# Delta branch of a hybrid mixer kernel: the two 64 x 64 squares of a block's diagonal stored side by side

## What is computed

```
G = cumsum(g) ; decay = where(j <= i, exp(G_i - G_j), 0)
m = where(j < i, (k*beta) k^T * decay, 0) ; a = m + I           # 64 x 64
u, w = solve_triangular(a, [v*beta, k*beta*exp(G)])             # unit lower
attn = (q k^T) * decay                                          # 64 x 64
per chunk: v_new = u - w S ; o = q exp(G) S + attn v_new ; S = S exp(G_last) + k_tail^T v_new
```

## Time and profile before

| what | value |
|---|---|
| median of 3 runs | 1843.88 us (1841.74 to 1844.7) |
| the profiled execution: its time | 1846.73 us |
| the profiled execution: its span, first to last instruction | 1844.9 us |
| mean granted TensorE clock | 0.997 |
| VectorE busy | 1250.9 us, 68% |
| ScalarE busy | 952.7 us, 52% |
| GpSimd busy | 315.0 us, 17% |
| HBM read | 302.90 MB, 165 GB/s over the span |

### The profile page before, as it was taken

The page is one execution under the profiler, slowest core; times in us unless marked ns, Lnnn a source line. Parts: engine busy times, 40 slices in busy tenths (PEclk is TensorE's granted clock), DMA queues, the critical chain, the costliest instruction groups (busy, mean ns, idle before and its releaser), DMA issues.

```text
span 1844.9 us, 37214 instructions
## 1 busy us (share of the span) xinstructions
PE 1805.4 (98%) x15880; PEld 1714.5 (93%) x15880; DVE 1250.9 (68%) x1668; ACT 952.7 (52%) x1377; POOL 315.0 (17%) x174
## 2 busy tenths in 40 slices
PE   7999999999999999999999999999999999999998
PEld 7889998998888999999989999999999889999998
DVE  6885677665689648777648775587647795677643
ACT  5634466544554345564545445556534545556533
POOL 0050231000002303200001453320001352321000
PEclk9999999999999999999999999999999999999999
DMA  6453354656445334655665563456655654445663
GB/s 242 154 167 104 124 174 157 204 193 210 154 149 172 116 115 140 203 177 180 195 196 169 192 206 126 138 178 199 202 191 174 224 188 131 140 168 195 195 196 102
DMA packets 91524, 315.54 MB, mean 171 GB/s; under 512 B 11616, under 2 KB 12768, under 8 KB 91104
## 3 DMA queue, kind: packets, MB, share of 16 engines
q1 hardware_dynamic: 90784, 312.60, 52.3%
q10 hardware_dynamic: 576, 0.57, 0.1%
HBM read 302.90 MB, written 1.05 MB: 165 GB/s over the span
## 4 chain that ended last, share of the span: by engine, by line
PE 84%; DVE 12%; ACT 3%; issue 1%; DMA 0%; SPq 0%; DVEq 0%; ACTq 0%
PE bank L2019 82%; DVE wlo L1144 4%; DVE area L1144 3%; DVE area L1150 2%; ACT area L648 1%; ACT whi L654 1%; PE bank L2613 1%; DVE hl L1150 1%; DVE xT L1150 1%; DMA raw<-in_weights 0%; DVE area L1664 0%; DVE area L1662 0%; PE bank L2634 0%; PE bank L2253 0%; ACT L636 0%
## 5 line engine op out<-in xcount | busy, mean ns | idle before, releaser
L1144 DVE TENSOR_TENSOR wlo<-raw,whi 128x1024 fp32r<-128x1024 f32 x514 | 665.7, 1309 | 388.3 <-ACT whi L654 387.6
L2019 PE MATMUL bank<-hh,whi 128*128 128x256 f32 x2896 | 818.6, 284 | 23.8 <-DVE wlo L1144 18.7
L2019 PE MATMUL bank<-hh,wlo 128*128 128x256 f32 x2906 | 802.1, 277 | 0.0
L2019 PE MATMUL bank<-hl,whi 128*128 128x256 f32 x2896 | 794.4, 278 | 0.0
L654 ACT CAST whi<-raw 128x1024 fp32r<-128x1024 f32 x568 | 585.3, 1047 | 373.3 <-PE bank L2019 324.1
L2019 PEld LDWEIGHTS bank<-hh,whi 128*128 128x128 f32 x2896 | 545.6, 188 | 40.5 <-DVE wlo L1144 23.1
L2019 PEld LDWEIGHTS bank<-hh,wlo 128*128 128x128 f32 x2906 | 546.3, 188 | 0.0
L2019 PEld LDWEIGHTS bank<-hl,whi 128*128 128x128 f32 x2896 | 541.6, 189 | 1.5 <-issue 1.4
L1800 POOL TENSOR_TENSOR area<-area 128x512 f32<-128x512 f32 (+4 forms) x84 | 138.3, 1652 | 535.4 <-ACT area L648 213.3
L1800 POOL TENSOR_TENSOR wlo<-raw,whi 128x1024 fp32r<-128x1024 f32 x54 | 138.4, 2564 | 385.2 <-ACT whi L654 385.2
L2019 PE MATMUL bank<-FH,whi 128*128 128x256 f32 x640 | 177.4, 277 | 0.0
(11 more groups left out here) (132 smaller groups left out, 1905.9 us busy)
## 6 DMA issues: line engine op xcount, KB each, us to landing
raw<-in_weights SPq DMA_DIRECT2D x568, 512.0 KB, 4.1
area<-area SPq DMA_DIRECT2D x100, 64.0 KB, 3.8
area<-area SPq DMA_DIRECT2D x16, 128.0 KB, 4.0
cst<-in_const SPq DMA_DIRECT2D x1, 1188.0 KB, 8.1
cst<-in_const SPq DMA_DIRECT2D x1, 1024.5 KB, 5.8
xT<-in_x SPq DMA_DIRECT2D x4, 256.0 KB, 7.3
out<-xT SPq DMA_DIRECT2D x4, 256.0 KB, 2.8
area<-in_lev SPq DMA_DIRECT2D x2, 384.0 KB, 6.9
```

What stands on the lines that cost most here:

```text
L1144: return v.tensor_tensor(dst, x, y, op)
L2019: return e.matmul(ps, x, y, start=start, stop=stop, skip_group_check=skip)
```

## The change

The 64 x 64 squares of the seven tiles are stored with both squares of a block in the same 64 columns: square 0 in partitions 0 to 63, square 1 in partitions 64 to 127, block b in columns 64b to 64b+63. Eight blocks take 512 columns: one PSUM bank and half a tile. Every VectorE and ScalarE operation on those tiles now covers 512 columns, and the pairs of operations over j become one with one wait. The exception is the first difference out of the `cums` banks, which keep blocks of 128 columns: there two operations of 128 x 512 become four of 64 partitions x 256 columns. Matmuls of the groups are the same in number, size and order, with other addresses; their 16 results go to one bank, and they signal once in place of once per half. `KT`, `KB`, `VB`, `W` and `U` keep their form. The masks are stored in the same way; of the six transposed level masks only the first, the one that is used, is still loaded, so the constant transfer shrinks from 1188 KB to 128 x 1800 fp32 and each load of the level masks from 128 x 768 to 128 x 384 fp32. No instruction changes its place on any engine's list.

The diff, cut to its core:

```diff
+def cells(t):
+    return t[:, 0:512]
+def v8(t):
+    return t[:, 0:512].rearrange("p (b t) -> p b t", t=64)
...
 # ScalarE
-                act(DT[:, :], DT[:, :], AF.Exp).then_inc(*a_dn.up("decay", L))
+                act(cells(DT), cells(DT), AF.Exp).then_inc(*a_dn.up("decay", L))
...
-                for j in range(2):
-                    a.wait_ge(*e_dn.at("MT", L, j))
-                    a.copy(pair(MT, j), bank[j][:, :]).then_inc(*a_dn.up("MT", L, j))
+                a.wait_ge(*e_dn.at("MT", L))
+                a.copy(cells(MT), bank[0][:, :]).then_inc(*a_dn.up("MT", L))
...
-                        for j in range(2):
-                            a.wait_ge(*e_dn.at("XT", L, s, j))
-                            a.copy(pair(Y, j), bank[2 + j][:, :]).then_inc(*a_dn.up("Y", L, s, j))
+                        a.wait_ge(*e_dn.at("XT", L, s))
+                        a.copy(cells(Y), bank[2][:, :]).then_inc(*a_dn.up("Y", L, s))
...
 # VectorE
-                    tt(quarter(pair(DT, j)), quarter(bank[j]), wide(G_[:, 4 * j:4 * j + 4], 2, 128), OP.subtract).then_inc(*v_dn.up("d", L, j))
+                    for q in range(2):
+                        r = slice(64 * q, 64 * q + 64)
+                        x = tt(v8(DT)[r, 4 * j:4 * j + 4, :], quarter(bank[j])[r, :, r], wide(G_[r, 4 * j:4 * j + 4], 2, 64), OP.subtract)
+                    x.then_inc(*v_dn.up("d", L, j))
...
-                tt(v3(DT, 128), v3(DT, 128), wide(C("upper"), 1, 8), OP.mult).then_inc(*v_dn.up("diff", L))
+                tt(v8(DT), v8(DT), wide(C("tri"), 1, 8), OP.mult).then_inc(*v_dn.up("diff", L))
...
-                for j in range(2):
-                    v.wait_ge(*e_dn.at("KK", L, j))
-                    tt(quarter(pair(M, j)), quarter(bank[j]), wide(be[:, 4 * j:4 * j + 4], 2, 128), OP.mult).then_inc(*v_dn.up("m", L, j))
-                    v.wait_ge(*v_dn.now())
-                    v.wait_ge(*e_dn.at("DT", L, j))
-                    tt(pair(M, j), pair(M, j), bank[2 + j][:, :], OP.mult).then_inc(*v_dn.up("M", L, j))
+                v.wait_ge(*e_dn.at("KK", L))
+                tt(v8(M), v8(bank[0]), wide(be, 2, 64), OP.mult).then_inc(*v_dn.up("m", L))
+                v.wait_ge(*v_dn.now())
+                v.wait_ge(*e_dn.at("DT", L))
+                tt(cells(M), cells(M), bank[2][:, :], OP.mult).then_inc(*v_dn.up("M", L))
...
-                tt(v3(X, 128), v3(M, 128), wide(lev(0), 1, 8), OP.mult).then_inc(*v_dn.up())
+                tt(v8(X), v8(M), wide(lev(0), 1, 8), OP.mult).then_inc(*v_dn.up())
...
-                    for j in range(2):
-                        v.wait_ge(*e_dn.at("LX", L, s, j))
-                        tt(quarter(pair(T0, j)), quarter(bank[j]), wide(lev(s), 1, 4), OP.mult).then_inc(*v_dn.up("T0", L, s, j))
+                    v.wait_ge(*e_dn.at("LX", L, s))
+                    tt(v8(T0), v8(bank[0]), wide(lev(s), 1, 8), OP.mult).then_inc(*v_dn.up("T0", L, s))
...
-                    for j in range(2):
-                        v.wait_ge(*e_dn.at("XLX", L, s, j))
-                        tt(pair(t, j), pair(t, j), bank[b + j][:, :], OP.subtract).then_inc(*v_dn.up("X", L, s, j))
+                    v.wait_ge(*e_dn.at("XLX", L, s))
+                    tt(cells(t), cells(t), bank[b][:, :], OP.subtract).then_inc(*v_dn.up("X", L, s))
...
 # TensorE
+            def cell(t, b, q):
+                return t[64 * q:64 * q + 64, 64 * b:64 * b + 64]
-            def sub_blocks(name, x, y, b0):
-                for j in range(2):
-                    for b in range(4 * j, 4 * j + 4):
-                        for q in range(2):
-                            o = mm(sub(bank[b0 + j], b % 4, q), sub(x, b, q), sub(y, b, q), True, True, True)
-                    o.then_inc(*e_dn.up(*name, j))
+            def sub_blocks(name, x, y, to):
+                for b in range(8):
+                    for q in range(2):
+                        o = mm(cell(bank[to], b, q), cell(x, b, q), cell(y, b, q), True, True, True)
+                o.then_inc(*e_dn.up(*name))
...
```

More of the change, by code:

```diff
@@ L43 @@
     ("ones", 128), ("eye", 128), ("eps6", 1), ("eps5", 1), ("one", 1), ("pad", 1),
-    ("upper", 128), ("chunk", 128), ("levT", 6 * 128),
+    ("upper", 128), ("chunk", 128), ("levT", 64), ("tri", 64), ("unit", 64),
     ("cos", 256), ("sin", 256), ("rmask", 4 * 128), ("xi", 4 * 64), ("zeta", 4), ("cnt", 4 * 16), ("cntw", 4)])
@@ L377, in program @@
         SM = slot(16)
-        LEV = SM[:, 256:1024]
+        LEV = SM[:, 256:640]
         Z = slot(17)
@@ L1279, in delta @@
                 v.wait_ge(*v_dn.now())
[L1280 removed]
+                tt(v8(X), v8(M), wide(lev(0), 1, 8), OP.mult).then_inc(*v_dn.up())
                 v.wait_ge(*v_dn.now())
[L1282 to L1284 removed]
+                stt(v8(X), v8(X), -1.0, wide(C("unit"), 1, 8), OP.mult, OP.add).then_inc(*v_dn.up("X", L, 0))
+                v.wait_ge(*a_dn.at("MT", L))
+                tt(v8(Y), v8(MT), wide(C("levT"), 1, 8), OP.mult).then_inc(*v_dn.up())
                 v.wait_ge(*v_dn.now())
[L1286 removed]
+                stt(v8(Y), v8(Y), -1.0, wide(C("unit"), 1, 8), OP.mult, OP.add).then_inc(*v_dn.up("Y", L, 0))
                 yield 1
[L1288 to L1290 removed]
+                v.wait_ge(*e_dn.at("KQ", L))
+                tt(cells(AT), cells(DT), bank[2][:, :], OP.mult).then_inc(*v_dn.up("AT", L))
                 yield 1
                 for s in range(1, 6):
[L1293 to L1295 removed]
+                    v.wait_ge(*e_dn.at("LX", L, s))
+                    tt(v8(T0), v8(bank[0]), wide(lev(s), 1, 8), OP.mult).then_inc(*v_dn.up("T0", L, s))
                     yield 1
@@ L2265, in sub, with sub_turned, sub_scores @@
                 return t[64 * q:64 * q + 64, 128 * b + 64 * q:128 * b + 64 * q + 64]
-            def sub_turned(name, src, b0):
-                for j in range(2):
-                    for b in range(4 * j, 4 * j + 4):
-                        for q in range(2):
-                            x = mm(sub(bank[b0 + j], b % 4, q), sub(src, b, q), sub(C("eye"), 0, q), True, True, True)
-                    x.then_inc(*e_dn.up(*name, j))
-            def sub_blocks(name, x, y, b0):
-                for j in range(2):
-                    for b in range(4 * j, 4 * j + 4):
-                        for q in range(2):
-                            o = mm(sub(bank[b0 + j], b % 4, q), sub(x, b, q), sub(y, b, q), True, True, True)
-                    o.then_inc(*e_dn.up(*name, j))
[L2283 to L2290, removed]
+            def cell(t, b, q):
+                return t[64 * q:64 * q + 64, 64 * b:64 * b + 64]
+            def sub_turned(name, src, to):
+                for b in range(8):
+                    for q in range(2):
+                        x = mm(cell(bank[to], b, q), cell(src, b, q), sub(C("eye"), 0, q), True, True, True)
+                x.then_inc(*e_dn.up(*name))
+            def sub_blocks(name, x, y, to):
+                for b in range(8):
+                    for q in range(2):
+                        o = mm(cell(bank[to], b, q), cell(x, b, q), cell(y, b, q), True, True, True)
+                o.then_inc(*e_dn.up(*name))
+            def sub_scores(name, x, y, to):
+                for b in range(8):
+                    for q in range(2):
+                        c = slice(128 * b + 64 * q, 128 * b + 64 * q + 64)
+                        o = mm(cell(bank[to], b, q), x[:, c], y[:, c], True, True, True)
+                o.then_inc(*e_dn.up(*name))
             def fresh2(b0, event):
@@ L2359, in delta @@
                         r = slice(64 * q, 64 * q + 64)
-                        x = mm(bank[q][:, 64 * b:64 * b + 64], KB[r, 128 * b:128 * b + 128], sub(Y, b, q), True, True, True)
+                        x = mm(bank[q][:, 64 * b:64 * b + 64], KB[r, 128 * b:128 * b + 128], cell(Y, b, q), True, True, True)
                         if b == 7:
@@ L2367, in delta @@
                             r, c = slice(64 * q, 64 * q + 64), 128 * (b % 4)
-                            x = mm(bank[2 + j][r, c:c + 128], sub(Y, b, q), VB[r, 128 * b:128 * b + 128], True, True, True)
+                            x = mm(bank[2 + j][r, c:c + 128], cell(Y, b, q), VB[r, 128 * b:128 * b + 128], True, True, True)
                     x.then_inc(*e_dn.up("U", L, j))
@@ L2404, in delta @@
                         for d in (0, 64):
-                            x = mm(place(h)[d:d + 64, :], hv(VN)[r, h, d:d + 64], AT[r, 128 * b + 64 * q:128 * b + 64 * q + 64], n == 0, True, True)
+                            x = mm(place(h)[d:d + 64, :], hv(VN)[r, h, d:d + 64], AT[r, 64 * b:64 * b + 64], n == 0, True, True)
                     x.then_inc(*e_dn.up("o", L, n))
@@ L2676, in levels, with cells_of @@
     return [(p // (2 << s) == f // (2 << s)) & (p // (1 << s) % 2 == 1) & (f // (1 << s) % 2 == 0) for s in range(6)]
+def cells_of(a):
+    return np.concatenate([a[0:64, 0:64], a[64:128, 64:128]], 0)
 def constants1():
@@ L2695, in constants1 @@
     put("chunk", same)
-    lev = levels()
```

(6 more changed lines are left out.)

36 lines of the change are left out of this document (18 added, 18 removed).

## The result

| kernel | median | runs |
|---|---|---|
| before | 1843.85 us | 1841.74 to 1844.7 |
| changed | 1872.72 us | 1871.44 to 1873.57 |

The ratio is 1.016, with a 95% interval of 1.0147 to 1.0172: the change makes the kernel slower by 29 us, where 8 us less was forecast. The profiled execution has a span of 1870.2 us and a mean granted clock of 0.999.

A forecast was written before the change was run, and what follows sets the result against it. VectorE was taken to bound layer 0's delta branch until 112.9 us, then TensorE's weight matmuls. Stalls and tails of 3.96 + 4.15 us, together 8.1, off the median 1843.88 gave 1835.8 us; range 1833.5 to 1840.0.

The forecast's parts named there:

- The stall and its removal: TensorE waits 2.58 us before `XLX` of level 1 in both layers; with slow-clock tails 8.1 us, all to go.
- the critical `T0`: VectorE's mask of `T0` at level 1, for which TensorE waits; to end 5.6 us earlier, 3.1 us spare.
- the rule on the shared ports: GpSimd and two-SBUF-input VectorE operations take turns; second subtraction would end at 107.0 us, `T0` at 108.8, 1.6 us spare.
- the two stretches: 114 to 116 and 598 to 600 us, behind the stalls; TensorE's granted clock to rise from 0.50 to 1.00.
- The four operations of 64 x 256: VectorE's first difference, four operations replacing two of 128 x 512: 1.64 us against 1.19, adding 0.45 us.
- The sum of 8.1 us: Stalls and slow-clock tails on TensorE, 3.96 us in layer 0 plus 4.15 in layer 1, all saved.
- 8.1 + 2 us off: The largest saving in the range of 8 in 10, whose lower end was given as 1833.5 us.
- the row: Profile times of VectorE's subtractions: 2.24 us beside GpSimd against 1.22, 1.0 us dearer; one more leaves 2.1 us spare.
- The step that failed: TensorE's own work, 18 groups of 32 records, taken at unchanged price.
- The rival on the slow side: TensorE's groups get dearer as squares share bank columns; doubled, +1.08 us each over 36 groups: 1874.7 us, chance 0.05.
- the rule on row tiles and banks: Different row tiles can't write the same PSUM bank at once, so a block's two squares would take turns.
- The other rivals: Part of the stall stays (one whole layer's: 1839.8 us), chance 0.10; time reappears at the next wait, 1843.9 us, chance 0.06.

The follow-up runs named there:

- run 1: The changed kernel with the constant tile padded back to 2636 columns, so the tiles behind it start where they did before: 1833.35 us, ratio 0.9961.
- run 3: The changed kernel with the constant tile 8 columns longer (2317 in place of 2309): 1831.67 us, ratio 0.9956.
- run 10: The kernel of run 3 with nine more VectorE operations of 512 columns, on columns nothing reads, ahead of `Y` in each layer: 1842.62 us, ratio 1.0018.
- run 6: The kernel of run 3 with `whi` and `wlo` moved 64 bytes on, `hh`, `hl` and the region 128: 1881.5 us, ratio 1.0221.
- run 5: The kernel of run 3 with every tile in SBUF, weights included, moved 64 bytes on: 1832.87 us, ratio 0.9953.
- run 2: The kernel before with its constant tile 8 columns (32 bytes) longer and nothing else: 1875.58 us, ratio 1.0187.
- run 7: The kernel of run 3 with `hh`, `hl` and the region moved 128 bytes on: 1857.14 us, ratio 1.0091.

## Why the prediction was wrong

**The stall and its removal: right.** The steps on VectorE can be read in the kernel with 8 columns more, where the place of tiles does not disturb. Its list of VectorE operations ahead of the critical `T0`:

```profile
102.25 1.22 DVE L1150 TENSOR_TENSOR wlo<-raw,whi 128x1024 fp32r<-128x1024 f32 x1
103.39 0.68 DVE L1150 TENSOR_TENSOR area<-area,bank 128x512 f32<-128x512 f32 x1
103.99 2.83 DVE L1150 TENSOR_TENSOR wlo<-raw,whi 128x1024 fp32r<-128x1024 f32 x1
106.74 1.87 DVE L1150 TENSOR_TENSOR area<-bank,area 128x512 f32<-128x512 f32 x3
```

GpSimd's first operation there, and TensorE with the group that had stood still:

```profile
103.34 2.40 POOL L1805 TENSOR_TENSOR area<-area 128x1024 f32<-128x1024 f32 x1 [102.92 <-PE bank L2024]
```

```profile
105.96 1.15 PE L2024 MATMUL bank<-area 64*64 64x64 f32 x32
107.04 0.50 PE L2024 MATMUL bank<-whi,hh 128*128 128x512 f32 x1
...
110.89 1.15 PE L2024 MATMUL bank<-area 64*64 64x64 f32 x32
111.96 0.50 PE L2024 MATMUL bank<-whi,hh 128*128 128x512 f32 x1
...
114.92 1.15 PE L2024 MATMUL bank<-area 64*64 64x64 f32 x32
```

`T0` ends at 106.74 + 1.87 = 108.61 us, in the foretold 107 to 109.5, and TensorE takes it at 110.89 us with 2.3 us to spare; 3.1 were forecast and 1.6 by the rule on the shared ports. TensorE itself got there 0.4 us later than in the kernel before (110.45 us), and `LX` of level 2 starts 3.5 us earlier (118.45 us, now 114.92), where 4 were forecast. The granted clock in the two stretches is 1.00 in place of 0.50:

```profile
114.00:116.00 2.00, 2.00 (x41) 1.55 (x41) 1.10 (x1) 0.00 (x0) 1.99 (x1) 1.00 0.26 78
598.00:600.00 2.00, 2.00 (x10) 1.65 (x9) 1.45 (x2) 0.23 (x1) 2.00 (x2) 1.00 0.82 260
```

The four operations of 64 x 256 took 1.74 us (82.88 to 84.62 in the changed kernel), 1.64 forecast. The sum of 8.1 us came out as 8.4 (run 1) and 10.1 us (run 3), both with intervals that hold 8.1 but are 5 to 6 us wide, so the closeness of 8.4 is partly luck; run 10 gives back 10.0, for stalls longer than the old ones. The range's lower end, "8.1 + 2 us off", would be 1833.8 us; the 1833.5 that stands there decides nothing.

**GpSimd and the ports: foreseen by the rule more closely than by the row.** GpSimd started at 103.34 us (102.7 forecast), and the subtraction beside it took 2.83 us and ended at 106.82; the price from the row, 2.24 us, would have had it end at 106.2, the rule of the Trainium skill, page "SBUF — State Buffer", section "SBUF: two separate sides", at 107.0. GpSimd's operation of 2.40 us ended at 105.74, and the subtraction 1.1 us later, as it did behind GpSimd in the kernel before. Part of the hit is luck: the working had GpSimd start at 102.6 us and take the 3.2 us of the earlier trace rows; it started 0.7 us later and took 0.8 us less.

VectorE's busy time fell by 13 us where 21 were forecast. Subtractions beside GpSimd explain little of it: the busy time of all 514 weight subtractions on VectorE is 665.7 us on the page of the kernel before, 669.5 in the changed kernel and 664.9 in run 3, where VectorE's total fell by 17 us. Where the rest stayed is open.

**The step that failed** is the last sentence on what lies under other work: "TensorE's own work is the same 18 groups of 32 records; I take its price as unchanged, and bound it below." The groups are unchanged, and the bound was drawn for the groups alone. The price of the other 11,600 matmuls was put at nothing without a reason. The diff had it in a line about constants: a table that became shorter moved `hh`, `FH` and all between by 1312 bytes against `whi`. Each kernel against the kernel before on its own chip, that cost 28.9 + 8.4 = 37.3 us, give or take 4 us by the two intervals: 28.9 us that the changed kernel lost, and the 8.4 us that run 1 shows it to have saved.

**The rival on the slow side gave 1874.7 us, within 2 us of the measurement, for the wrong reason.** It had the groups of 64 x 64 doubled in price through squares that share columns of a bank. They cost 1.08 us in the changed kernel as in the kernel before, and in run 3 (105.96 to 107.04 us), so the rule on row tiles and banks that stood beside it decided nothing here: squares in the same columns of a bank take no longer than squares side by side. Its own sign, a group longer than 1.1 us, is absent; the time alone would have confirmed it.

**The other rivals** did not occur: no idle of TensorE replaced the stall, and no part of it stayed.

## What to carry to other kernels

A change of a table's length or a tile's shape is also a change of every address behind it. Before the saving of such an edit is judged, pin the base of the tiles behind it (here one line), or compute the starts of the moving and the stationary operand before and after; and when all matmuls of a kernel slow down by a few per cent at full clock and without idle time, compare addresses before instructions. The best kernel here is the changed one with 8 columns of padding, 1831.67 us; it beats both.

## What the runs showed of the hardware

The pace of a stream of 128 x 128 by 256 fp32 matmuls depends on the distance in SBUF between the tile being streamed and the tile from which weights are loaded: 112.8 ns at a remainder of 192 modulo 256, 118.3 at 160, 119.5 at 0, all in the stretch of 340 to 400 us. In time of this kernel the spread is 1831.7 to 1889.2 us. The Trainium skill, page "TensorE: Matmul & The Clock Gate", section "Step-by-step: what each phase is for", says that TensorE has two independent read ports, so that loading the next weights takes no read bandwidth from the running matmul. The runs don't bear that out as it stands: with both operands in place it may be so, but moving the weights by 64 bytes against the moving operand (run 6) costs 49 us over run 5, where both moved together. That reads of both meet in one part of the memory is a guess; no run shows the mechanism.

The granted clock fell to 0.50 behind idle stretches of TensorE of 2.58 us (kernel before, both layers) and of 3.51 and 3.37 us (run 10), and stayed at 1.00 behind those of 1.11 and 1.12 us in run 2.

Open are the shape of the table (why 192 and not 64, and whether 32 is good), why matmuls with 512 columns of weights moving follow another order, and a change of pace at one distance: run 7 has both paces in one execution, and the kernel before is not always at its best either. In a later stretch, the feed-forward projection of layer 1 at 880 to 900 us, it began 172 matmuls in 20 us, 116.3 ns each, and the changed kernel 173, so nothing was lost there.
